# Merge stage: the first four row tiles are formed together, block of features by block of features, with four y buffers

## The chip, the core and the metric

The kernel runs on one core of one Trainium2 chip. The metric is the device time of one execution in microseconds (us). The kernel before took 2590.55 us, the median of three executions (2588.41 to 2590.64).

## What is computed

Two post-norm layers of a streaming encoder over 2048 positions of 1024 features. Each layer ends in the same step: a mixer's gated output is multiplied by an output matrix, the result is added to the scaled residual, and each position is normalised. In the reference:

```
# layer 0 (attention):      h = einsum("bse,ed->bsd", o * silu(gate), w_out)
# layer 1 (RG-LRU):         h = einsum("bse,ed->bsd", y, w_out)
x = layer_norm(DEEPNORM_ALPHA * x + h, ln_g[layer], ln_b[layer])

def layer_norm(x, g, b):
    mu = mean(x);  var = mean(square(x - mu))
    return (x - mu) * rsqrt(var + LN_EPS) * g + b
```

Everything is float32. A float32 product is made of three products of split halves: high times high, high times low, low times high.

## The kernel before

The program is a row of stages, each a block with a barrier at its end: `project`, `attend`, `merge` ("ma"), `project_recur` ("rep"), `merge` again ("rem"). The change touches `merge` alone (lines 796 to 944), which runs twice. It reads the mixer's output as two halves (high and low) laid out features by positions, and the 1024x1024 output matrix, and writes 2048x1024 rows.

Positions are cut into 16 row tiles of 128 (`ST` = 16), features into 8 blocks of 128 (`KC` = 8), output columns into two halves of 512 (`DH` = 2). One row tile takes 8 x 2 x 3 = 48 matmuls and fills two PSUM banks (one `psum[u]`, u = tile mod 4); four such pairs fill all eight banks.

SyncE (queue SP) loads, in this order (lines 841 to 849): weight blocks 0 and 1 (1 MB), y of row tiles 0 and 1 (all 8 feature blocks, both halves, 2 MB, into `yin[0]`), weight blocks 2 and 3, y of tiles 2 and 3 (`yin[1]`), weight blocks 4 and 5, 6 and 7, four tiles of x (0.5 MB each), gain and shift. ScalarE makes the high half of each weight pair (line 908), VectorE the low half (line 920). TensorE then forms tile 0 over all its feature blocks, waiting at each pair of blocks for its split (line 889), then tile 1, and so on: one tile after another, each over all eight blocks.

Behind each tile VectorE adds the residual (line 929), takes the statistics and normalises (lines 933 to 943, with a root on ScalarE), GpSimd multiplies by the gain and adds the shift (lines 877 and 879), and SyncE stores the tile (line 855). After every odd tile n SyncE issues the y of tiles n+3 and n+4 (line 859, 2 MB) right behind the store, then waits until the store has landed (line 861), and reloads the x buffer (line 862). TensorE's tile n waits for its y and for VectorE's sum of tile n-4, which frees its PSUM pair (lines 885 and 886). TensorE, ScalarE, VectorE, GpSimd and SyncE loop over groups of four tiles with a hardware loop.

Of the kernel before, what the change touches and what calls it, by code (L numbers as in the profile page):

```python
# [19 lines left out]
P = 128  # L20
BANK = 512
ALU = mybir.AluOpType
ACT = mybir.ActivationFunctionType
F32 = mybir.dt.float32
F32R = mybir.dt.float32r
# [29 lines left out]
def raw(ap):  # L55

    return ap.bitcast(F32)
# [346 lines left out]
def wait(engine, sem, value):  # L404

    if not isinstance(value, int) or value > 0:
        engine.wait_ge(sem, value)
# [388 lines left out]
def merge(nc, stage, ys, w_out, x, ln_g, ln_b, out):  # L796
# [3 lines left out]
    DH = D // BANK  # L800
# [6 lines left out]
    with ExitStack() as ctx:  # L807
# [1 line left out]
        wst = a.sb("wst", [P, KC, D])  # L809
        wh = a.sb("wh", [P, KC, D], F32R)  # L810
        wl = a.sb("wl", [P, KC, D], F32R)
        yin = [a.sb(f"yin{i}", [P, 2, KC, YW], F32R) for i in range(2)]
        xt = a.sb("xt", [P, RING, D])
        gain = a.sb("gain", [P, D])
        shift = a.sb("shift", [P, D])
# [3 lines left out]
        psum = [a.ps(f"ps{i}", [P, DH, BANK]) for i in range(4)]  # L819

        w_loaded = [a.sem(f"w_loaded{i}") for i in range(WP)]
        p_loaded = a.sem("p_loaded")
        y_loaded = [a.sem(f"y_loaded{i}") for i in range(2)]
        x_loaded = [a.sem(f"x_loaded{i}") for i in range(RING)]
# [14 lines left out]
        @block.sync  # L839
        def _(sp):  # L840
            for h in range(WP):
                part = slice(h * CP, (h + 1) * CP)
                sp.dma_start(wst[:, part, :], w_v[:, part, :]).then_inc(w_loaded[h], 16)  # L843
                if h < 2:
                    sp.dma_start(raw(yin[h][:, :, :, :]), y_v[:, :, :, h * YW:(h + 1) * YW]).then_inc(y_loaded[h], 16)  # L845
            for u in range(RING):
                sp.dma_start(xt[:, u, :], x[u * P:(u + 1) * P, :]).then_inc(x_loaded[u], 16)
            for v, row in ((gain, ln_g), (shift, ln_b)):
                sp.dma_start(v[:, :], row.partition_broadcast(P)).then_inc(p_loaded, 16)

            def tiles(it, last):
                for u in range(RING):
                    n = it * RING + u
                    sp.wait_ge(shifted, n + 1)
                    sp.dma_start(out[bass.ds(n * P, P), :], xt[:, u, :]).then_inc(stored[u], 16)
                    if not last:
                        if u % 2 == 1:
                            b = u // 2
                            sp.dma_start(raw(yin[b][:, :, :, :]), y_v[:, :, :, bass.ds((n + 3) * P, YW)])\
                                .then_inc(y_loaded[b], 16)  # L860
                        sp.wait_ge(stored[u], 16 * (it + 1))
                        sp.dma_start(xt[:, u, :], x[bass.ds((n + RING) * P, P), :]).then_inc(x_loaded[u], 16)

            with sp.Fori(0, ST // RING - 1) as it:
                tiles(it, False)
            tiles(ST // RING - 1, True)
            for u in range(RING):
                sp.wait_ge(stored[u], 16 * (ST // RING))

# [10 lines left out]

        @block.tensor
        def _(pe):
            def tile(it, u):
                n = it * RING + u
                pe.wait_ge(y_loaded[u // 2], 16 * (it + 1))
                wait(pe, summed, n - 3)
                for c in range(KC):
                    if isinstance(it, int) and u == 0 and c % CP == 0:
                        pe.wait_ge(w_split, c // CP + 1)
                    for h in range(DH):  # L890
                        for k, (l, w) in enumerate(((0, wh), (0, wl), (1, wh))):
                            mm = nc.tensor.matmul(psum[u][:, h, :], yin[u // 2][:, l, c, u % 2 * P:(u % 2 + 1) * P],  # L892
                                                  w[:, c, h * BANK:(h + 1) * BANK], start=(c == 0 and k == 0),
                                                  stop=(c == KC - 1 and k == 2))
                mm.then_inc(products, 1)

            for u in range(RING):
                tile(0, u)
            with pe.Fori(1, ST // RING) as it:
                for u in range(RING):  # L900
                    tile(it, u)

        @block.scalar
        def _(act):
            for h in range(WP):
                part = slice(h * CP, (h + 1) * CP)
                act.wait_ge(w_loaded[h], 16)
                nc.scalar.activation(wh[:, part, :], wst[:, part, :], ACT.Copy).then_inc(w_high, 1)  # L908

            with act.Fori(0, ST // RING) as it:  # L910
                for u in range(RING):
                    act.wait_ge(stat, (it * RING + u + 1) * (DH + 2))
                    nc.scalar.activation(rstd[:, u % 2, 0:1], mean_var[:, u % 2, 1:2], ACT.Sqrt).then_inc(rooted, 1)  # L913

        @block.vector
        def _(dve):
            for h in range(WP):
                part = slice(h * CP, (h + 1) * CP)
                dve.wait_ge(w_high, h + 1)
                nc.vector.tensor_tensor(wl[:, part, :], wst[:, part, :], raw(wh[:, part, :]), ALU.subtract)\  # L920
                    .then_inc(w_split, 1)

            with dve.Fori(0, ST // RING) as it:
                for u in range(RING):
# [598 lines left out]
```

## Time and profile before

| | |
|---|---|
| median of 3 executions | 2590.55 us (2588.41 to 2590.64) |
| profiled execution | 2593.75 us, of which the span is 2591.9 us |
| TensorE matmul busy | 2417.6 us (93%), 13921 instructions |
| VectorE, ScalarE, GpSimd busy | 1339.5, 1156.4, 623.0 us |
| mean granted TensorE clock | 0.969 |

A profile is one execution. Its engines are PE (TensorE matmul), PEld (TensorE weight load), DVE (VectorE), ACT (ScalarE), POOL (GpSimd) and SPq (SyncE's queue, which issues the DMAs). Times in the views count from the start of the span. The granted clock is a share of full speed: 1.00 is 2.4 GHz and 0.50 is 1.2 GHz. Matmul starts are recorded, their ends are modelled, so the spacing of starts says more than the duration of one. The first merge lies from 1655 to 1866 us, the second from 2382 to 2592 us.

### The profile page before, as it was taken

What the parts mean: (1) busy time and instruction counts of PE and PEld (TensorE: products, weight loads), DVE (VectorE), ACT (ScalarE), POOL (GpSimd) and SP (SyncE); (2) the same over time, 40 slices, a digit from 0 to 9 for tenths busy, and PEclk for the clock granted to TensorE, in tenths of its full rate; (3) what the DMA queues carried; (4) which work ended last, traced back from release to release, by engine and by line L of the source; (5) the groups of instructions that cost most, each with busy time, mean ns of one, the idle gap of its engine ahead of it and who ended that gap; (6) DMA issues with size and microseconds to landing.
All of it is one profiled execution on the core that took longest, in us unless ns stands there. A gap on an engine that the chain in (4) does not pass through costs nothing. (4 is left out here: it accounts for less than half of the span.)

```text
span 2591.9 us, 41884 instructions
## 1 busy us (share of the span) xinstructions
PE 2417.6 (93%) x13921; PEld 2086.2 (80%) x13921; DVE 1339.5 (52%) x2832; ACT 1156.4 (45%) x2128; POOL 623.0 (24%) x740
## 2 busy tenths in 40 slices
PE   8899999999997999999999999599689999993898
PEld 7688889998876888898888988488578888872786
DVE  4312121211007888888888888433245666574333
ACT  4211111111116888888888888400034556575000
POOL 0000000000002555455545555234300000000244
PEclk9999999999998999999999999799899999996999
DMA  5344343332116445544454444545344354435553
GB/s 182 112 114 130 114 128 107 123 113 86 52 49 146 98 97 126 128 97 96 111 128 111 96 98 95 181 159 194 122 147 122 127 158 130 138 123 168 195 191 135
DMA packets 215772, 325.65 MB, mean 126 GB/s; under 512 B 16097, under 2 KB 141089, under 8 KB 209441
## 3 DMA queue, kind: packets, MB, share of 16 engines
q1 hardware_dynamic: 215136, 323.68, 43.4%
q8 instruction: 53, 0.87, 0.1%
q0 software_dynamic: 512, 0.53, 0.1%
q14 instruction: 71, 0.57, 0.1%
HBM read 197.79 MB, written 126.35 MB: 125 GB/s over the span
## 5 line engine op out<-in xcount | busy, mean ns | idle before, releaser
L760 DVE TENSOR_TENSOR at_pl<-at_tps,at_ph 128x512 fp32r<-128x512 f32 (+3 forms) x640 | 371.0, 604 | 21.7 <-ACT at_ph L705 21.5
L705 ACT ACTIVATE at_ph<-at_tps 128x512 fp32r<-128x512 f32 (+3 forms) x640 | 312.3, 528 | 108.6 <-PE at_tps L627 104.7
L323 ACT ACTIVATE pa_stg<-pa_ps 128x512 fp32r<-128x512 f32 (+1 forms) x128 | 76.2, 597 | 608.1 <-PE pa_ps L227 608.1
L627 PE MATMUL at_tps<-at_ident,at_probs 128*128 128x128 f32 x2176 | 338.3, 273 | 1.4 <-DVE at_pl L760 1.4
L642 PE MATMUL at_ops<-at_ph,at_val 128*128 128x256 f32 (+1 forms) x1152 | 325.1, 304 | 2.0 <-DVE at_pl L760 1.9
L227 PE MATMUL pa_ps<-pa_xh,pa_wh 128*128 128x512 f32 x800 | 312.9, 391 | 12.1 <-DVE pa_stg L390 9.6
L695 ACT ACTIVATE at_probs<-at_probs,at_least 128x128 f32<-128x128 f32 (+15 forms) x256 | 307.1, 1200 | 18.9 <-DVE at_probs L751 18.8
L227 PE MATMUL pa_ps<-pa_xl,pa_wh 128*128 128x512 f32 x800 | 312.2, 390 | 0.0
L227 PE MATMUL pa_ps<-pa_xh,pa_wl 128*128 128x512 f32 x800 | 312.2, 390 | 0.0
L612 PE MATMUL at_sps<-at_k,at_q 128*128 128x512 f32 (+3 forms) x640 | 272.2, 425 | 26.1 <-DMA at_k<-forget_sums 22.1
L642 PE MATMUL at_ops<-at_pl,at_val 128*128 128x256 f32 (+1 forms) x1152 | 294.8, 281 | 0.0
L627 PEld LDWEIGHTS at_tps<-at_ident,at_probs 128*128 128x128 f32 x2176 | 256.1, 141 | 25.0 <-DVE at_pl L760 6.8
L751 DVE TENSOR_SCALAR_CACHE_REDUCE at_probs<-at_sps,at_least 128x512 f32<-128x512 f32 (+3 forms) x384 | 248.2, 646 | 16.7 <-PE at_sps L613 0.5
L613 PE MATMUL at_sps<-at_k,at_q 68*128 68x512 f32 (+3 forms) x640 | 233.4, 368 | 0.0
L642 PEld LDWEIGHTS at_ops<-at_ph,at_val 128*128 128x128 f32 x1152 | 220.5, 191 | 12.2 <-issue 2.5
L642 PEld LDWEIGHTS at_ops<-at_pl,at_val 128*128 128x128 f32 x1152 | 219.8, 191 | 8.3
L1230 PE MATMUL rep_ps<-rep_xh,rep_wh 128*128 128x512 f32 x512 | 201.6, 394 | 2.9 <-DVE rep_wl L1369 2.9
L751 DVE TENSOR_SCALAR_CACHE_REDUCE at_probs<-at_sps 128x512 f32<-128x512 f32 (+3 forms) x256 | 162.1, 633 | 79.2 <-PE at_sps L613 54.9
L892 PE MATMUL rem_ps<-rem_wh,rem_yin 128*128 128x512 f32 x512 | 161.9, 397 | 43.3 <-DMA rem_yin<-y_gated 36.4
L1230 PE MATMUL rep_ps<-rep_xh,rep_wl 128*128 128x512 f32 x512 | 200.6, 392 | 0.0
L1230 PE MATMUL rep_ps<-rep_xl,rep_wh 128*128 128x512 f32 x512 | 200.4, 391 | 0.0
L393 DVE TENSOR_TENSOR pa_stg<-pa_ps,pa_stg 128x512 fp32r<-128x512 f32 x64 | 44.3, 691 | 286.5 <-ACT pa_stg L323 286.5
(165 smaller groups left out, 4664.2 us busy)
## 6 DMA issues: line engine op xcount, KB each, us to landing
at_q<-q_halves SPq DMA_DIRECT2D x48, 512.0 KB
at_k<-k_halves SPq DMA_DIRECT2D x48, 512.0 KB
pa_wst<-in_attn_w_in SPq DMA_DIRECT2D x16, 1024.0 KB, 7.2
q_halves<-pa_stg SPq DMA_DIRECT2D x32, 512.0 KB, 3.7
k_halves<-pa_stg SPq DMA_DIRECT2D x32, 512.0 KB, 3.7
v_halves<-pa_stg SPq DMA_DIRECT2D x32, 512.0 KB, 2.8
at_val<-v_halves SPq DMA_DIRECT2D x16, 1024.0 KB, 16.8
ma_yin<-y_halves SPq DMA_DIRECT2D x8, 2048.0 KB, 9.0
```

The source lines that it names most:

```text
L227: mm = nc.tensor.matmul(out, lhs[p](c), rhs[q](c), start=(c == 0 and k == 0), stop=(c == KC - 1 and k == 2))
L323: nc.scalar.activation(out, source(kind, s), func, scale=scale).then_inc(evac_h, 1)
L612: nc.tensor.matmul(out, q1[hp][:, i * P:(i + 1) * P], k1[hp][:, keys], start=True, stop=False)
L613: mm = nc.tensor.matmul(out, q2[hp][0:K, i * P:(i + 1) * P], k2[hp][0:K, keys], start=False, stop=not last)
L627: mm = nc.tensor.transpose(tps[c % TB][:, k, :], probs[s % ROWS][:, t0:t0 + P], ident[:, :])
L642: mm = nc.tensor.matmul(ops[b][:, 0, c0:GW], val[hp][:, kt, :], t[b][:, kt, c0:GW], start=(kt == 0 and t is ph), stop=(kt == KT - 1 and t ...
L695: nc.scalar.activation(probs[s % ROWS][:, 0:w], probs[s % ROWS][:, 0:w], ACT.Exp, bias=least[:, s % ROWS, n_chunks[s] - 1:n_chunks[s]], sc ...
L705: nc.scalar.activation(ph[g % 2][:, j * PB:j * PB + n, i % 2 * P:(i % 2 + 1) * P], tps[c % TB][:, 0:n, :], ACT.Copy).then_inc(high_out, 1)
L751: nc.vector.tensor_scalar(probs[s % ROWS][:, j * BANK:j * BANK + w], sps[c % SB][:, 0:w], 1.0, least[:, s % ROWS, j - 1:j] if j else None, ...
L760: nc.vector.tensor_tensor(pl[g % 2][at], tps[c % TB][:, 0:n, :], raw(ph[g % 2][at]), ALU.subtract)\
L892: mm = nc.tensor.matmul(psum[u][:, h, :], yin[u // 2][:, l, c, u % 2 * P:(u % 2 + 1) * P], w[:, c, h * BANK:(h + 1) * BANK], start=(c == 0 ...
L1230: mm = nc.tensor.matmul(psum[t % RING][:, :], wt[:, b, k, :], xt[:, k, at], start=(k == 0 and m == 0), stop=(k == KC - 1 and m == 2))
```

## The change

Weights are loaded in single blocks of 128 features, and so is the y of the first four tiles: for each pair of blocks two weight transfers (0.5 MB each), then four y transfers (one block, two tiles, both halves: 0.25 MB each). TensorE forms tiles 0 to 3 together: for block 0 all four tiles' products, then block 1, and so on, with all eight PSUM banks open. The weight split is made block by block (8 steps each on ScalarE and VectorE, where there were 4). There are four y buffers; y of tiles 4 to 7 is issued in front, behind x, gain and shift. After that y of tiles n+3 and n+4 is issued after odd tiles n = 5, 7, 9, 11, and now behind the x reload, so behind the wait for the store. TensorE's and SyncE's loops over tiles are written out.

```diff
-        yin = [a.sb(f"yin{i}", [P, 2, KC, YW], F32R) for i in range(2)]
+        yin = [a.sb(f"yin{i}", [P, 2, KC, YW], F32R) for i in range(4)]
...
+        y_first = [a.sem(f"y_first{i}") for i in range(WP)]
...
             for h in range(WP):
-                part = slice(h * CP, (h + 1) * CP)
-                sp.dma_start(wst[:, part, :], w_v[:, part, :]).then_inc(w_loaded[h], 16)
-                if h < 2:
-                    sp.dma_start(raw(yin[h][:, :, :, :]), y_v[:, :, :, h * YW:(h + 1) * YW]).then_inc(y_loaded[h], 16)
+                for c in range(h * CP, (h + 1) * CP):
+                    sp.dma_start(wst[:, c, :], w_v[:, c, :]).then_inc(w_loaded[h], 16)
+                for c in range(h * CP, (h + 1) * CP):
+                    for b in range(2):
+                        sp.dma_start(raw(yin[b][:, :, c, :]), y_v[:, :, c, b * YW:(b + 1) * YW]).then_inc(y_first[h], 16)
...
-            def tiles(it, last):
-                for u in range(RING):
-                    n = it * RING + u
-                    sp.wait_ge(shifted, n + 1)
-                    sp.dma_start(out[bass.ds(n * P, P), :], xt[:, u, :]).then_inc(stored[u], 16)
-                    if not last:
-                        if u % 2 == 1:
-                            b = u // 2
-                            sp.dma_start(raw(yin[b][:, :, :, :]), y_v[:, :, :, bass.ds((n + 3) * P, YW)])\
-                                .then_inc(y_loaded[b], 16)
-                        sp.wait_ge(stored[u], 16 * (it + 1))
-                        sp.dma_start(xt[:, u, :], x[bass.ds((n + RING) * P, P), :]).then_inc(x_loaded[u], 16)
...
+            def load_y(j):
+                sp.dma_start(raw(yin[j % 4][:, :, :, :]), y_v[:, :, :, j * YW:(j + 1) * YW]).then_inc(y_loaded[j % 2], 16)
+
+            load_y(2)
+            load_y(3)
+            for n in range(ST):
+                u = n % RING
+                sp.wait_ge(shifted, n + 1)
+                sp.dma_start(out[n * P:(n + 1) * P, :], xt[:, u, :]).then_inc(stored[u], 16)
+                if n + RING < ST:
+                    sp.wait_ge(stored[u], 16 * (n // RING + 1))
+                    sp.dma_start(xt[:, u, :], x[(n + RING) * P:(n + RING + 1) * P, :]).then_inc(x_loaded[u], 16)
+                if n % 2 == 1 and RING <= n < ST - RING:
+                    load_y((n + 3) // 2)
...
+            def part(n, c):
+                u = n % RING
+                for h in range(DH):
+                    for k, (l, w) in enumerate(((0, wh), (0, wl), (1, wh))):
+                        mm = nc.tensor.matmul(psum[u][:, h, :], yin[n // 2 % 4][:, l, c, n % 2 * P:(n % 2 + 1) * P],
+                                              w[:, c, h * BANK:(h + 1) * BANK], start=(c == 0 and k == 0),
+                                              stop=(c == KC - 1 and k == 2))
+                return mm
+
+            def tile(n):
+                pe.wait_ge(y_loaded[n // 2 % 2], 16 * (n // RING))
+                pe.wait_ge(summed, n - 3)
                 for c in range(KC):
...
+                    mm = part(n, c)
                 mm.then_inc(products, 1)
...
+            for c in range(KC):
+                pe.wait_ge(w_split, c + 1)
+                pe.wait_ge(y_first[c // CP], 32 * CP)
                 for u in range(RING):
-                    tile(it, u)
+                    mm = part(u, c)
+                    if c == KC - 1:
+                        mm.then_inc(products, 1)
+            for n in range(RING, ST):
+                tile(n)
...
+            for c in range(KC):
+                act.wait_ge(w_loaded[c // CP], 16 * CP)
+                nc.scalar.activation(wh[:, c, :], wst[:, c, :], ACT.Copy).then_inc(w_high, 1)
...
+            for c in range(KC):
+                dve.wait_ge(w_high, c + 1)
+                nc.vector.tensor_tensor(wl[:, c, :], wst[:, c, :], raw(wh[:, c, :]), ALU.subtract).then_inc(w_split, 1)
```

## Rows read from the trace of the kernel before

**Rows 1.** The page's costliest groups: busy us, mean ns, idle before, releaser.
```profile
L892 PE MATMUL rem_ps<-rem_wh,rem_yin 128*128 128x512 f32 x512 | 161.9, 397 | 43.3 <-DMA rem_yin<-y_gated 36.4
```

**Rows 2.** TensorE's waits: who waited for whom, us in total, times, longest.
```profile
PE rem_ps L892 <- DMA rem_yin<-y_gated: 36.4, 1, 36.4
...
PE ma_ps L892 <- DMA ma_yin<-y_halves: 19.5, 1, 19.5
...
PE ma_ps L892 <- DVE ma_wl L920: 8.3, 2, 7.0
...
PE rem_ps L892 <- DVE rem_wl L920: 6.9, 2, 5.6
```

**Rows 3.** Timeline, head of the first merge: start, us, engine, line, operation.
```profile
1655.14 0.40 SPq L843 DMA_DIRECT2D ma_wst<-in_attn_w_out  x1
1655.60 0.45 SPq L845 DMA_DIRECT2D ma_yin<-y_halves  x1
...
1660.12 1.91 ACT L908 ACTIVATE ma_wh<-ma_wst 128x2048 fp32r<-128x2048 f32 x1 [12.30 <-DMA ma_wst<-in_attn_w_out]
...
1662.07 2.29 DVE L920 TENSOR_TENSOR ma_wl<-ma_wst,ma_wh 128x2048 fp32r<-128x2048 f32 x1 [19.78 <-ACT ma_wh L908]
1666.13 0.29 PEld L892 LDWEIGHTS ma_ps<-ma_wh,ma_yin 128*128 128x128 f32 x1 [19.77 <-DMA ma_yin<-y_halves]
...
1672.99 0.50 PE L892 MATMUL ma_ps<-ma_wh,ma_yin 128*128 128x512 f32 x1 [1.37 <-DVE ma_wl L920]
...
1683.01 0.79 PE L892 MATMUL ma_ps<-ma_wh,ma_yin 128*128 128x512 f32 x1 [6.98 <-DVE ma_wl L920]
```

**Rows 4.** Windows, first merge: busy (count) per engine, granted clock, DMA share, GB/s.
```profile
1655.00:1660.00 5.00, 0.00 (x0) 0.00 (x0) 0.00 (x0) 0.00 (x0) 0.00 (x0) 0.50 0.75 245
1660.00:1665.00 5.00, 0.00 (x0) 0.00 (x0) 2.29 (x1) 1.91 (x1) 0.00 (x0) 0.50 1.10 356
1665.00:1670.00 5.00, 3.87 (x9) 3.09 (x10) 0.00 (x0) 1.29 (x1) 0.00 (x0) 0.50 1.06 380
1670.00:1675.00 5.00, 3.63 (x13) 2.36 (x13) 2.29 (x1) 0.61 (x1) 0.00 (x0) 0.78 1.09 363
...
1685.00:1690.00 5.00, 5.00 (x22) 4.09 (x21) 0.52 (x1) 0.00 (x0) 0.00 (x0) 0.91 0.37 147
```

**Rows 5.** The chain that ended last, head of the second merge: start, us, what.
```profile
2382.25 0.38 SPq L843
...
2408.68 170.94 PE rem_ps L892 x744
2579.63 0.02 issue
2579.65 1.23 DVE rem_xt L929
```

**Rows 6.** Timeline: residual sums of tiles 0, 1 and 15, and tile 0's gain.
```profile
1690.11 1.22 DVE L929 SCALAR_TENSOR_TENSOR ma_xt<-ma_xt,ma_ps 128x1024 f32<-128x1024 f32 x1 [4.59 <-PE ma_ps L892]
...
1694.55 2.39 POOL L877 TENSOR_TENSOR ma_xt<-ma_xt,ma_gain 128x1024 f32<-128x1024 f32 x1 [42.98 <-DVE ma_xt L943]
...
1700.99 1.22 DVE L929 SCALAR_TENSOR_TENSOR ma_xt<-ma_xt,ma_ps 128x1024 f32<-128x1024 f32 x1 [6.51 <-PE ma_ps L892]
...
1853.31 1.22 DVE L929 SCALAR_TENSOR_TENSOR ma_xt<-ma_xt,ma_ps 128x1024 f32<-128x1024 f32 x1 [6.51 <-PE ma_ps L892]
```

**Rows 7.** Timeline of SyncE's queue: stores, x reloads and y refill behind tiles 0 and 1.
```profile
1699.60 0.37 SPq L855 DMA_DIRECT2D x<-ma_xt  x1
1702.42 0.35 SPq L862 DMA_DIRECT2D ma_xt<-in_x  x1
1710.47 0.35 SPq L855 DMA_DIRECT2D x<-ma_xt  x1
1711.01 0.39 SPq L859 DMA_DIRECT2D ma_yin<-y_halves  x1
```

**Rows 8.** Line L859, all 12 y refills of both merges: issue to landing.
```profile
DMA to landing us min/median/max: 8.8/8.9/10.2
```

**Rows 9.** Windows at the program's start, where x comes in 0.5 MB transfers.
```profile
6.00:9.00 3.00, 3.00 (x16) 2.98 (x15) 2.43 (x5) 2.24 (x4) 0.00 (x0) 1.00 1.01 379
9.00:12.00 3.00, 1.90 (x13) 1.52 (x11) 2.53 (x5) 2.18 (x5) 0.00 (x0) 1.00 1.07 379
```

More of the change, by code:

```diff
@@ L849, in _ @@
                 sp.dma_start(v[:, :], row.partition_broadcast(P)).then_inc(p_loaded, 16)
-            def tiles(it, last):
-                for u in range(RING):
-                    n = it * RING + u
-                    sp.wait_ge(shifted, n + 1)
-                    sp.dma_start(out[bass.ds(n * P, P), :], xt[:, u, :]).then_inc(stored[u], 16)
-                    if not last:
-                        if u % 2 == 1:
-                            b = u // 2
-                            sp.dma_start(raw(yin[b][:, :, :, :]), y_v[:, :, :, bass.ds((n + 3) * P, YW)])\
-                                .then_inc(y_loaded[b], 16)
-                        sp.wait_ge(stored[u], 16 * (it + 1))
-                        sp.dma_start(xt[:, u, :], x[bass.ds((n + RING) * P, P), :]).then_inc(x_loaded[u], 16)
-            with sp.Fori(0, ST // RING - 1) as it:
-                tiles(it, False)
-            tiles(ST // RING - 1, True)
+            def load_y(j):
[11 more added lines that the diff above has]
+                    load_y((n + 3) // 2)
             for u in range(RING):
@@ L882, in _ @@
         def _(pe):
[L883 to L886, printed above, removed]
-                for c in range(KC):
[L888 to L894, printed above, removed]
+            def part(n, c):
[6 more added lines that the diff above has]
+                return mm
@@ L895, in tile @@
+            def tile(n):
+                pe.wait_ge(y_loaded[n // 2 % 2], 16 * (n // RING))
+                pe.wait_ge(summed, n - 3)
+                for c in range(KC):
+                    mm = part(n, c)
                 mm.then_inc(products, 1)
-            for u in range(RING):
-                tile(0, u)
-            with pe.Fori(1, ST // RING) as it:
+            for c in range(KC):
+                pe.wait_ge(w_split, c + 1)
+                pe.wait_ge(y_first[c // CP], 32 * CP)
                 for u in range(RING):
-                    tile(it, u)
+                    mm = part(u, c)
+                    if c == KC - 1:
+                        mm.then_inc(products, 1)
@@ L903, in _ @@
+            for n in range(RING, ST):
+                tile(n)
         @block.scalar
         def _(act):
[L905 to L908, printed above, removed]
+            for c in range(KC):
+                act.wait_ge(w_loaded[c // CP], 16 * CP)
+                nc.scalar.activation(wh[:, c, :], wst[:, c, :], ACT.Copy).then_inc(w_high, 1)
@@ L916, in _ @@
         def _(dve):
[L917 to L921, printed above, removed]
+            for c in range(KC):
+                dve.wait_ge(w_high, c + 1)
+                nc.vector.tensor_tensor(wl[:, c, :], wst[:, c, :], raw(wh[:, c, :]), ALU.subtract).then_inc(w_split, 1)
             with dve.Fori(0, ST // RING) as it:
```

## The prediction

> **What bounds the kernel now.** I began with the page. TensorE is busy 93% of the span, so only time in which it stands still, or runs at the low clock, is there to be won; the page's group for line 892 shows 43.3 us of idle time in the second merge alone [rows 1]. TensorE's waits say what that is: it waits once per merge for y, and twice per merge for the split of the weights [rows 2]. The long y waits (36.4 and 19.5 us) are mostly the end of the stage before and the barrier; what the change can reach begins with the merge's first DMA issue, at 1655.14 and 2382.25. So I went to the timeline of the head. TensorE starts at 1666.13, 11.0 us after the first issue, runs two feature blocks of tile 0, starts the next two at 1672.99 and the last four only at 1683.01 [rows 3]. The windows show why: until 1675 the DMA engines are full (share 1.06 to 1.10, 356 to 380 GB/s) [rows 4], and tile 0 needs all the weights, the last in the queue. From there on nothing stops TensorE: the residual sums of tiles 0 and 15 start at 1690.11 and 1853.31, 163.20 us for 15 tiles, 10.88 us a tile, and tiles 0 to 1 show the same 10.88 [rows 6]. The second merge is alike: after the weights' last wait, one unbroken piece of TensorE work, 744 of the 768 matmuls, from 2408.68 to 2579.63 [rows 5]. The tail behind the last product (sum, norm, gain, shift, store) is untouched.
>
> In sum: 16 tiles are 16 x 10.88 = 174.1 us of work at the full clock. The first merge takes 1853.31 - 1655.14 = 198.2 us from first issue to last product, the second 2579.65 - 2382.25 = 197.4 us. So 24.1 and 23.3 us are start, gaps and low clock.
>
> **The start.** The change moves TensorE's first matmul to where one pair of blocks has landed: weights 1.05 MB and y 1.05 MB, 2.10 MB in all, instead of 3.15 MB. By 1660 some 5 x 0.245 = 1.23 MB have moved, by 1665 3.01 MB [rows 4], by 1666.13 (1.13 us at 0.380) 3.43 MB, when the 3.15 MB asked for have landed [rows 3]; 0.28 MB of later transfers lay between them. With the same 0.28 MB the new first pair has landed when 2.38 MB have moved: 1660 + (2.38 - 1.23) / 0.356 = 1663.2, 8.1 us after the first issue. The split isn't in the way: the first weights land at 1660.12, ScalarE takes 1.91 and VectorE 2.29 us for two blocks [rows 3], so about half for one: block 0 is split near 1660.1 + 1.0 + 1.2 = 1662.3, block 1 near 1663.5, while block 0 holds TensorE 24 matmuls, 5.4 us and more. Eight short steps instead of four long ones cost nothing behind that cover; without it they cost their fixed parts, under a us.
>
> **The gaps.** Afterwards each pair of blocks is 48 matmuls, 10.9 us of TensorE time, and takes 2.10 MB / 0.36 to 0.38 = 5.5 to 5.8 us to arrive. The transfers gain 5 us a pair and both gaps go. Behind the 8.4 MB stand 2 MB of x, 1 MB of gain and shift and now 4.2 MB of y for tiles 4 to 7: 15.7 MB at 0.38 are 41 us, done near 1698, needed from 1663.2 + 2.3 + 4 x 10.88 = 1709. The 24 head issues (6 before) cost 0.40 to 0.45 us each [rows 3], 10.5 us, less than the 22 us in which their bytes move.
>
> The kernel before runs tile 0 in three bursts with waits between them, and the clock is 0.50 until 1670 and low again at 1683 [rows 3, 4]; after the change a burst (10.9 us) is longer than the arrival behind it (5.5 to 5.8), so there should be one burst only. A rule of the Trainium skill (TensorE: Matmul & The Clock Gate, HAM oscillation) speaks against the new shape: do all K-tiles of one row tile before waiting for data, since short bursts between DMA waits bring the low clock back, and the change does one K block of four tiles at a time. By that rule the low clock would return at each later pair; that is rival F.
>
> **The clock.** The head before is slow twice. From 1666.13 the granted clock is 0.50, with 0.78 as mean of 1670 to 1675: 2.2 us more, so 6.1 us at half. At 1683.01, after 7 us of rest, it is low again until 1685.9 (0.91 as mean of 1685 to 1690) [rows 3, 4]: 2.9 us. The loss shows directly: 744 matmuls from 1683.01 at 10.88/48 us end at 1851.65, the sum starts at 1853.31, 1.7 us later; in the second merge 2408.68 + 168.64 = 2577.32 against 2579.65, 2.3 us. After the change there is one slow stretch: between 1.7 us and half of 6.1, 3.1 us. I take 2.3.
>
> **Ends.** First merge: 1663.2 + 174.1 + 2.3 = 1839.6 for 1853.31, 13.7 us. Second: 2382.25 + 8.1 + 174.1 + 2.3 = 2566.8 for 2579.65, 12.9 us. Together 26.6 us, with both ends' rows in [rows 3, 5, 6].
>
> **PSUM and the post-processing.** In the last feature block each tile takes 6 matmuls, so the first four tiles end 6 x 10.88/48 = 1.36 us apart and not 10.88; tile 0's last product comes 18 matmuls, 4.1 us, before tile 3's. Tile 4 needs tile 0's sum, 1.22 us [rows 6]: covered with 2.8 us to spare. VectorE needs some 4.4 us a tile (1690.11 to GpSimd's start at 1694.55), GpSimd 4.8: counted from tile 0's last product, GpSimd ends tiles 0 to 3 near 9.4, 14.2, 19.1 and 23.9, and tile 5's product comes at 4.1 + 21.8 = 25.9. The queue has drained by then; SyncE's store, wait and reload of 3.2 us a tile fit too.
>
> **The y refill.** This is the new wait. Before, y of tiles n+3 and n+4 is issued 10.02 us after tile n's product (1711.01 - 1700.99), lands 8.9 us later [rows 6 to 8], and is needed 2 x 10.88 = 21.76 us after it: 2.8 us to spare. After, it stands behind the wait for the store and the x reload: store at 9.48, reload 2.82 later as for tile 0 (1702.42 - 1699.60) [rows 7], then y some 0.4 us later: 12.7, landing at 21.6, with 0.1 us to spare. Queued behind that wait on SyncE are y and nothing else urgent. Though there are four buffers, the refill is no earlier. The slowest refill took 10.2 [rows 8], which would be 1.2 us late. A late refill gives the next pair as much slack, so only two of the four refills of a merge can be late by the whole amount d: cost 2d a merge, 0 to 2 x 1.2. I take 0.5 us for both merges together, and 4.8 as the bound.
>
> Loops written out: tile ends 10.88 us apart are exactly 48 spacings of a loop body, so TensorE's loop costs nothing now and its removal gives nothing.
>
> **Sum.** 26.6 - 0.5 = 26.1 us. The profiled execution took 2593.75 us, span 2591.9 and 1.85 around it; less 26.1 that is 2567.6. The median of the executions lies 3.2 below the profiled one: 2590.55 - 26.1 = 2564.5.
>
> **Rivals.**
> A, late start. If the small transfers are slower or land interleaved with the next pair's, TensorE starts later. Price: if its first pair needs what 4.2 MB took before, it starts where the second pair of weights landed, about 1668.7 (split 4.3 us before 1672.99), 5.5 us late, two times: gain 26.1 - 11 = 15, 2575.5; halfway, gain 20.6, 2570. For it: a block of y is a quarter of a MB, and no row has that size in a stream. Against: 0.5 MB transfers in a row run at 379 GB/s [rows 9], as the large ones do. The Trainium skill (DMA: Bandwidth & Descriptors, Measured) asks for transfers of 1 MiB or more for 75% of the peak; 379 GB/s in 0.5 MB pieces doesn't bear it out for a stream.
> B, late refills. All at 10.2 us to landing: d = 1.1, cost 2 x 2 x 1.1 = 4.4, and for each wait perhaps a lower clock: gain 22, 2568.5.
> C, slower than before. The same refill behind x: if reload and refill hinder each other so that y lands d late, the cost is 4d in all; it eats the 26.6 us at d = 6.7 and is a loss over 0.2% (5.2 us) at d = 8, y landing 17 us after its issue. Price at d = 8: +5.4, 2596. Against: no refill took over 10.2.
> D, the change doesn't do what it says: the pieces are issued singly, but they land all together and TensorE stands until nearly the last, near 1683. Then all 768 matmuls come behind 1683 and not 744, and 24 x 10.88/48 = 5.4 us are lost per merge: 2590.5 + 10.9 = 2601; a start up to 5.4 us before that is no loss, 2590.
> F, low clock at each pair. If TensorE comes to stand between pairs long enough, each of the three later pairs of a merge costs a slow stretch of at least 1.7 us, 2 x 3 x 1.7 = 10.2 in all: gain 15.9, 2574.7. Against: it needs a pair to arrive later than 10.9 us behind the last one, and the arrivals take half of that [rows 4]. It is the skill's rule named above.
> E, better than forecast: start at 1662.4 (2.10 MB exactly), clock loss 1.7, no late refill: 26.6 + 2 x (0.8 + 0.6) = 29.4, 2561.
>
> **How the numbers follow.** Forecast, 2564.5 with its own 2562 to 2567: 0.48. E: 0.12. B: 0.14. A: 0.17. F: 0.02. C: 0.03. D: 0.04. The range runs from 2560 (E and the spread of executions, 1.5) to 2573 (B, and A past its middle), and leaves out about one in ten. A measurement tells about 0.2%, 5.2 us, from no change. Faster 0.93 (forecast, E, B, A, F), same 0.03 (part of C and D), slower 0.04.
>
> **What would show it.** In the profile after: the merge's first matmul 8.1 us behind its first weight issue; no gap until the last product; tile 4's first matmul without a wait; one stretch at half clock per merge; a wait for y at tile 8 under 1 us; last products near 1839.6 in the first merge and, with the time won there taken off, near 2566.8 - 13.7 = 2553.1 in the second. A start after 1666 would break the first step, y waits at tiles 8 and 12 over 1.2 us the refill step, a second low clock the clock step.

## The result, and the profile after

The changed kernel takes 2577.75 us (median of 6 executions, 2574.78 to 2579.05), the kernel before on the same chip 2590.6 us (6 executions). The ratio is 0.9946, 95% interval 0.9936 to 0.9957: 12.85 us faster, where 26.1 were forecast, and outside the range of 2560 to 2573. The direction is right, half of the gain is missing. Two executions far off all others (6372 us of the kernel before and 10166 us of before_refill_behind) are left out of the ratios below.

The profiled execution took 2578.18 us, with a span of 2576.3. Its timeline at the head of the first merge (start, us, engine, line, operation), to be read against [rows 3]:

```profile
1654.58 0.93 SPq L844 DMA_DIRECT2D ma_wst<-in_attn_w_out  x2
1655.55 1.99 SPq L847 DMA_DIRECT2D ma_yin<-y_halves  x4
1657.58 3.35 SPq L844 DMA_DIRECT2D ma_wst<-in_attn_w_out  x2
1659.84 2.01 ACT L913 ACTIVATE ma_wh<-ma_wst 128x1024 fp32r<-128x1024 f32 x2 [12.57 <-DMA ma_wst<-in_attn_w_out]
...
1667.46 0.77 PE L887 MATMUL ma_ps<-ma_wh,ma_yin 128*128 128x512 f32 x1 [21.42 <-DMA ma_yin<-y_halves]
```

TensorE starts 12.9 us behind the first issue. It was 11.0 before and forecast at 8.1. In the second merge it starts at 2385.81, 11.5 us behind the first issue at 2374.30. The first weights still arrive some 5 us behind the issue; it is y that is late. TensorE's start lies behind 1666, which the prediction named as the sign that its first step is broken. The windows (busy per engine, granted clock, DMA share, GB/s) answer to [rows 4]; the last line is of the second merge:

```profile
1655.00:1660.00 5.00, 0.00 (x0) 0.00 (x0) 0.00 (x0) 0.16 (x1) 0.00 (x0) 0.50 0.77 246
1660.00:1665.00 5.00, 0.00 (x0) 0.00 (x0) 2.36 (x2) 1.84 (x2) 0.00 (x0) 0.50 0.94 244
1665.00:1670.00 5.00, 2.54 (x6) 2.10 (x7) 0.00 (x0) 0.10 (x1) 0.00 (x0) 0.50 0.98 323
1670.00:1675.00 5.00, 5.00 (x17) 3.93 (x17) 2.36 (x2) 1.90 (x2) 0.00 (x0) 0.69 1.01 334
...
2379.00:2384.00 5.00, 0.00 (x0) 0.00 (x0) 2.36 (x2) 2.01 (x2) 0.00 (x0) 0.50 0.79 213
```

Where 356 GB/s flowed before, 244 and 213 flow now, and the DMA engines are busy for 0.94 and 0.79, not 1.10. From its first matmul to its wait at tile 8 TensorE has no gap, as forecast. The next loss stands in the timeline of VectorE's tile sums (line 932). From tile 5 on, spacings longer than 10.88 us are what to look for, as in [rows 6]; the lines are those of tiles 0, 4, 5, 7, 8 and 15:

```profile
1709.86 1.22 DVE L932 SCALAR_TENSOR_TENSOR ma_xt<-ma_xt,ma_ps 128x1024 f32<-128x1024 f32 x1 [23.79 <-PE ma_ps L887]
...
1730.66 1.21 DVE L932 SCALAR_TENSOR_TENSOR ma_xt<-ma_xt,ma_ps 128x1024 f32<-128x1024 f32 x1
1736.17 1.21 DVE L932 SCALAR_TENSOR_TENSOR ma_xt<-ma_xt,ma_ps 128x1024 f32<-128x1024 f32 x1
...
1757.46 1.22 DVE L932 SCALAR_TENSOR_TENSOR ma_xt<-ma_xt,ma_ps 128x1024 f32<-128x1024 f32 x1 [6.52 <-PE ma_ps L887]
1770.37 1.22 DVE L932 SCALAR_TENSOR_TENSOR ma_xt<-ma_xt,ma_ps 128x1024 f32<-128x1024 f32 x1 [8.54 <-PE ma_ps L887]
...
1847.93 1.22 DVE L932 SCALAR_TENSOR_TENSOR ma_xt<-ma_xt,ma_ps 128x1024 f32<-128x1024 f32 x1 [6.52 <-PE ma_ps L887]
```

The step from tile 7 to tile 8 is 12.91 us, 2.03 too long. Tiles 12 and 14 are 0.21 and 1.19 late too, tile 8 of the second merge 1.88 and its tile 14 0.04. TensorE's own row at tile 8 names the refill:

```profile
1757.03 0.39 PE L887 MATMUL ma_ps<-ma_wh,ma_yin 128*128 128x512 f32 x1
1759.13 0.50 PE L887 MATMUL ma_ps<-ma_wh,ma_yin 128*128 128x512 f32 x1 [1.71 <-DMA ma_yin<-y_halves]
```

The sum of the merges fits the medians. From first issue to last sum the first merge takes 1847.93 - 1654.58 = 193.35 us (198.17 before), the second 2564.04 - 2374.30 = 189.74 (197.40): 4.8 and 7.7, together 12.5 us of the 12.85. The two profiles' spans differ by 3 us more, outside the two stretches from first issue to last sum.

| term, both merges | forecast | measured | missing |
|---|---|---|---|
| start behind the first issue | 8.1 + 8.1 | 12.9 + 11.5 | 8.2 |
| late refills | 0.5 | 3.4 + 1.9 | 4.8 |
| low clock (rest of first matmul to last sum, less 174.1) | 2.3 + 2.3 | 3.0 + 2.2 | 0.6 |

### The profile page after: what moved, and what is told of

It reads as the page before. It is cut to its first block and busy times, and to the rows that moved or that the text cites. A ratio compares the mean times of both kernels' runs of the same rounds, so it can differ in the third digit from the quotient of the medians.

```text
span 2576.3 us, 41772 instructions
## 1 busy us (share of the span) xinstructions
PE 2410.6 (94%) x13921; PEld 2081.1 (81%) x13921; DVE 1350.7 (52%) x2840; ACT 1160.1 (45%) x2136; POOL 623.2 (24%) x740
## 5 line engine op out<-in xcount | busy, mean ns | idle before, releaser
L227 PE MATMUL pa_ps<-pa_xh,pa_wh 128*128 128x512 f32 x800 | 313.1, 391 | 12.1 <-DVE pa_stg L390 9.6
```

What stands on the lines that cost most here:

```text
L227: mm = nc.tensor.matmul(out, lhs[p](c), rhs[q](c), start=(c == 0 and k == 0), stop=(c == KC - 1 and k == 2))
```

## Experiments

Each kernel is compared with the kernel before on its own chip; where a text gives a time against the changed kernel, it is the difference of medians, though all but after_padded_again ran on chips where the kernel before took 1.0 us less (2589.5 to 2589.6). The table shows, from each profile, the first matmul behind the first issue and the summed lateness of tiles 4 to 15, for both merges.

| kernel | median us | ratio to before (95%) | start | tiles late |
|---|---|---|---|---|
| changed kernel | 2577.75 | 0.9946 (0.9936 to 0.9957) | 12.9, 11.5 | 3.4, 1.9 |
| refill_early | 2570.93 | 0.9927 (0.9913 to 0.9940) | 12.8, 12.0 | 0, 0 |
| gpsimd_light | 2575.89 | 0.9942 (0.9927 to 0.9958) | 13.4, 12.0 | 0.6, 4.1 |
| head_large | 2572.37 | 0.9932 (0.9919 to 0.9946) | 11.6, 9.4 | 3.3, 1.9 |
| before_split_y | 2591.39 | 1.0008 (0.9998 to 1.0017) | 12.9, 12.1 | 0, 0 |
| large_early | 2568.13 | 0.9917 (0.9903 to 0.9930) | 11.7, 9.4 | 0, 0 |
| pitch_padded | 2563.17 | 0.9896 (0.9881 to 0.9911) | 8.3, 8.2 | 0, 0 |
| before_refill_behind | 2595.55 | 1.0022 (1.0012 to 1.0031) | 11.0, 11.1 | 2.5, 1.9 |
| before_padded | 2589.14 | 0.9997 (0.9988 to 1.0007) | 11.2, 11.6 | 0, 0 |
| after_padded | 2569.16 | 0.9917 (0.9901 to 0.9934) | 10.1, 10.1 | 4.3, 1.5 |
| after_padded_again | 2566.47 | 0.9907 (0.9879 to 0.9936) | 8.4, 8.4 | 3.4, 1.6 |
| halves_apart | 2570.93 | 0.9929 (0.9912 to 0.9946) | 13.0, 11.6 | 0, 0 |
| padded_large | 2561.96 | 0.9895 (0.9880 to 0.9910) | 7.8, 7.7 | 0, 0 |

**refill_early.** The four buffers are used; the refills of tiles 8 to 15 stand behind tiles 1, 3, 5 and 7, in front of the wait for the store. They count on other semaphores than in the changed kernel, and TensorE's wait follows (these lines are left out).

```diff
...
                 sp.dma_start(out[n * P:(n + 1) * P, :], xt[:, u, :]).then_inc(stored[u], 16)
+                if n % 2 == 1 and n < ST // 2:
+                    load_y((n + 7) // 2)
                 if n + RING < ST:
...
-                if n % 2 == 1 and RING <= n < ST - RING:
-                    load_y((n + 3) // 2)
...
```

> The changed kernel with the y refills of tiles 8 to 15 moved: y of tiles 8 and 9 is issued after tile 1's store and ahead of the wait for it, then one after tiles 3, 5 and 7, so that the four buffers are used. Theory (late refills): TensorE's waits at tiles 8, 12 and 14 (2.0, 0.2 and 1.2 us in the first merge, 1.9 at tile 8 in the second) vanish and the time falls by 5.3 us, to 2572.5. The start of each merge stays late (12.9 and 11.5 us behind the first issue). Rival (the waits stand for contention among the transfers, which comes with any refill): waits of 1 to 2 us turn up at other tiles and the time stays within 1 us of 2577.75.

All waits behind the head are gone: from first matmul to last sum 175.8 and 176.0 us, which is 174.1 and 1.7 and 1.9 us of low clock. The time falls by 6.8 us (5.9 if each is taken against the kernel before on its own chip), a little more than the 5.3 of the profile's lateness. Late refills are shown as one of the two losses, and contention that comes with any refill is out as their cause. The early refills do have a price, which lies elsewhere: x reloads are issued up to 9.4 us behind their store and not 2.6 to 4.5, and in the first merge tile 5's sum waits 1.9 us for its x. The pause before tile 6's product, 4.8 us for VectorE in the changed kernel, absorbs it.

**gpsimd_light.** The gain and shift of tiles 0 to 5 on 8 columns only; GpSimd's loop is written out for it.

```diff
...
+                w = 8 if n < 6 else D
...
-                    nc.gpsimd.tensor_tensor(xt[:, u, :], xt[:, u, :], gain[:, :], ALU.mult).then_inc(gained, 1)
+                nc.gpsimd.tensor_tensor(xt[:, u, :w], xt[:, u, :w], gain[:, :w], ALU.mult).then_inc(gained, 1)
```

> The changed kernel, but gain and shift are applied to 8 of 1024 columns in tiles 0 to 5 of each merge (that part of the output is left out). Theory (VectorE and GpSimd slow each other down while they work at the same time, which they did not do before): VectorE's normalising step behind tiles 1 to 5 takes 0.81 us and not 2.05, the residual sums of tiles 0 to 4 stand 4.3 us apart and not 5.5, tile 5's store is issued some 5 us earlier, and the wait at tile 8 is gone: time 3 to 5 us lower. Rival (the normalising step is long because sums queue up in front of it): 2.05 us stays.

The mechanism holds for the normalising step. That step of tile 1, of the changed kernel and then of this one (timeline of VectorE):

```profile
1717.69 2.04 DVE L946 TENSOR_SCALAR ma_xt<-ma_xt,ma_mean_var,ma_rstd 128x1024 f32<-128x1024 f32 x1
```

```profile
1715.76 0.81 DVE L946 TENSOR_SCALAR ma_xt<-ma_xt,ma_mean_var,ma_rstd 128x1024 f32<-128x1024 f32 x1
```

The sums of tiles 0 to 4 stand 4.27 us apart and not 5.51, and tile 8 starts without a wait in both merges. The time does not follow: 1.9 us less, not 3 to 5. In the profile another refill was late: in the second merge tile 7's store, issued at 2480.13, landed late, and with the refill behind it tile 10 came 4.04 us late. SyncE's queue there:

```profile
2480.13 0.34 SPq L861 DMA_DIRECT2D out<-rem_xt  x1
2484.59 0.32 SPq L864 DMA_DIRECT2D rem_xt<-x  x1
2484.96 0.44 SPq L854 DMA_DIRECT2D rem_yin<-y_gated  x1
```

4.46 us passed from store to reload, where most reloads of this kernel's later tiles took 2.6: a refill behind the wait carries each swing of the store. What delayed this store no run tells. The wait itself was 2.11 us. The rest of the 4.04 is a fresh start and the low clock, which came back here and behind no other refill of these profiles. The window (TensorE busy, granted clock, DMA share, GB/s) and, below it, the one behind the wait of 2.07 us at tile 14 of after_padded:

```profile
2495.00:2500.00 5.00, 5.00 (x17) 0.66 0.33 107
```

```profile
1820.00:1825.00 5.00, 2.93 (x13) 1.00 0.32 124
```

At a mean of 0.66 five microseconds lose 1.7 us of work. So this kernel shows that GpSimd's overlap makes the wait at tile 8, and its time says little about what that wait costs.

**before_refill_behind.** The kernel before with the refill moved behind the reload, nothing else.

```diff
...
-                        if u % 2 == 1:
-                            b = u // 2
-                            sp.dma_start(raw(yin[b][:, :, :, :]), y_v[:, :, :, bass.ds((n + 3) * P, YW)])\
-                                .then_inc(y_loaded[b], 16)
                         sp.wait_ge(stored[u], 16 * (it + 1))
                         sp.dma_start(xt[:, u, :], x[bass.ds((n + RING) * P, P), :]).then_inc(x_loaded[u], 16)
+                        if u % 2 == 1:
+                            b = u // 2
+                            sp.dma_start(raw(yin[b][:, :, :, :]), y_v[:, :, :, bass.ds((n + 3) * P, YW)])\
+                                .then_inc(y_loaded[b], 16)
```

> The kernel before with one edit: the y refill is issued behind the wait for the store and the x reload, as in the changed kernel. Theory of the prediction (the place alone leaves 0.1 us to spare): waits of 0 to 0.5 us at tiles 4, 8 and 12, in all under 2 us in both merges, ratio 1.000 to 1.001; the wait of 2 us at tile 8 in the changed kernel then needs VectorE's backlog as well. Rival (the place alone costs it): 2 us at every second pair, 6 to 8 us in all, ratio 1.0025 or more.

Neither expectation holds. The refill is issued 12.81 us behind the product (1712.50 - 1699.69), as worked out, and lands 9.1 us later in the median (8.7 to 9.7) and not 8.9. That leaves the 0.1 us to spare negative. TensorE's waits are short, and yet the sums come 0.6 to 0.8 us late at six of the twelve pairs and 0.3 at one, 4.4 us in all: a short wait costs more than itself. The waits of TensorE in the first merge, us in total, times, longest:

```profile
PE ma_ps L892 <- DMA ma_yin<-y_halves: 1.2, 4, 0.4
```

Four waits of 0.3 on average against 2.5 us of lateness, some 0.3 us for each fresh start. So the place alone costs 4.4 us in the profile and 1.0022 in the ratio, whose interval reaches the rival's 1.0025; the medians lie 6.0 us apart, of which the lateness covers all but 1.6.

**before_split_y.** The kernel before, with each of the two 2 MB transfers of y at the head in 8 pieces.

```diff
...
-                    sp.dma_start(raw(yin[h][:, :, :, :]), y_v[:, :, :, h * YW:(h + 1) * YW]).then_inc(y_loaded[h], 16)
+                    for c in range(KC):
+                        sp.dma_start(raw(yin[h][:, :, c, :]), y_v[:, :, c, h * YW:(h + 1) * YW]).then_inc(y_first[h], 16)
...
```

> The kernel before, with the y of tiles 0 and 1 and of tiles 2 and 3 loaded in 8 transfers of one block (0.25 MB) each, not in one of 2 MB; nothing else is changed, TensorE still works tile by tile. Theory (small transfers): y of tiles 0 and 1 lands 2 to 4 us later than 11.0 us behind the first issue, each merge starts and ends that much later at most, ratio 1.000 to 1.003. Rival (the order of y and weights): start at 11.0 us as before, ratio 1.000, and the DMA share stays at 1.05 to 1.10.

The same bytes in the same order arrive 1.9 and 1.1 us later, and the rate dips for the first four microseconds of y only. Windows of the first merge:

```profile
1655.00:1657.00 2.00, 0.00 (x0) 0.00 (x0) 0.00 (x0) 0.00 (x0) 0.00 (x0) 0.50 0.98 395
1657.00:1659.00 2.00, 0.00 (x0) 0.00 (x0) 0.00 (x0) 0.89 (x1) 0.00 (x0) 0.50 0.86 245
1659.00:1661.00 2.00, 0.00 (x0) 0.00 (x0) 0.95 (x1) 1.02 (x1) 0.00 (x0) 0.50 0.92 259
1661.00:1663.00 2.00, 0.00 (x0) 0.00 (x0) 1.34 (x1) 0.00 (x0) 0.00 (x0) 0.50 1.08 360
```

So cutting y into single blocks costs by itself, without TensorE's new order. But the dip ends at 1661, when half of these blocks are still to come: from 1661 to 1665 four more single-block transfers of y are issued and 365 GB/s flow. A single block read from rows 8 KB apart is thus not slow at all times. The later start hardly counts here, since the last weights set this kernel's end: 1.0008.

**head_large.** Three transfers per pair of blocks and not six: weights 1 MB, y of each block for all four tiles 0.5 MB. The first two y buffers lie side by side, and the waits follow (these lines are left out).

```diff
...
-                for c in range(h * CP, (h + 1) * CP):
-                    sp.dma_start(wst[:, c, :], w_v[:, c, :]).then_inc(w_loaded[h], 16)
+                part = slice(h * CP, (h + 1) * CP)
+                sp.dma_start(wst[:, part, :], w_v[:, part, :]).then_inc(w_loaded[h], 16)
                 for c in range(h * CP, (h + 1) * CP):
-                    for b in range(2):
-                        sp.dma_start(raw(yin[b][:, :, c, :]), y_v[:, :, c, b * YW:(b + 1) * YW]).then_inc(y_first[h], 16)
+                    sp.dma_start(raw(yf[:, :, c, :]), y_v[:, :, c, 0:2 * YW]).then_inc(y_first[h], 16)
...
```

> The changed kernel with the same bytes in the same order for each pair of blocks, in 3 transfers and not 6: the two weight blocks in one of 1 MB, and each y block for all four tiles in one of 0.5 MB with rows of 2 KB (the first two y buffers lie side by side). Theory (small transfers let the 16 DMA engines drift apart and stand still, so that the last engine finishes the first pair late): the windows behind the first weights show the DMA share back at 1.0 or more (0.94 and 0.79 now), the first matmul comes 8 to 9 us behind the first issue and not 12.9 and 11.5, time 6 to 8 us lower, 2570 to 2572. Rival (the first pair is late because its y was just written or because single blocks lie badly in memory): start still 11 to 13 us behind the issue, time as now.

The time falls by 5.4 us, less than the theory wanted, and the start by 1.3 and 2.1 only. The windows spoke against it: once y begins, transfers of twice the size dip as deep, though for a shorter time. Second merge:

```profile
2376.00:2378.00 2.00, 0.00 (x0) 0.00 (x0) 0.00 (x0) 0.36 (x1) 0.00 (x0) 0.50 1.00 373
2378.00:2380.00 2.00, 0.00 (x0) 0.00 (x0) 1.27 (x2) 1.65 (x2) 0.00 (x0) 0.50 0.71 185
2380.00:2382.00 2.00, 0.00 (x1) 0.03 (x1) 1.09 (x1) 0.00 (x0) 0.00 (x0) 0.50 0.96 370
```

185 GB/s with rows of 2 KB in 0.5 MB transfers; the changed kernel, with rows of 1 KB in 0.25 MB, had 241, 170 and 259 GB/s in the three windows from 2378.00. Twice the size does not lift the rate in the dip (187 GB/s at its lowest in the first merge), it shortens the dip. My theory of small transfers fell here as the main cause. What both have in common is where they read: 128 rows of one block, 8 KB apart.

**large_early** joins both repairs.

> Both repairs at once: the 3 larger transfers per pair of blocks of head_large and the early refills of refill_early. If the two losses (late start, late refills) are separate, the gains add: start as in head_large (11.6 and 9.4 us behind the first issue), no wait behind it, 175.8 us from first to last product: 2571 less some 3.5, 2567 to 2568. Rival (head_large's gain came from something else than the start): 2570 to 2571 as refill_early.

2568.13 us and the starts of head_large, without late tiles: 9.6 us under the changed kernel, of the 12.2 that separate losses would add up to (6.8 + 5.4). The profiles show both repairs side by side; the medians show most of the sum.

**pitch_padded.** refill_early with one more edit, in the memory layout of y; it is read and written as before.

```diff
...
-    qs, ks, ys = (dram(n, (2, D, S)) for n in ("q_halves", "k_halves", "y_halves"))
+    qs, ks = (dram(n, (2, D, S)) for n in ("q_halves", "k_halves"))
+    ys = dram("y_halves", (2, D, S + 256))[:, :, 0:S]
...
-    ys = nc.dram_tensor("y_gated", (2, D, S), F32, kind="Internal").ap()
+    ys = nc.dram_tensor("y_gated", (2, D, S + 256), F32, kind="Internal").ap()[:, :, 0:S]
```

> refill_early, with the rows of the y tensor in memory 9 KB apart instead of 8 KB (256 unused positions behind each row); transfers, order and sizes as in refill_early. Theory M (the transfers of single blocks are slow because rows 8 KB apart, in two halves 8 MB apart, meet in the same part of the memory: the rate is 150 to 250 GB/s in that stretch in small and in large transfers alike): the rate there goes to 350 GB/s or more, the first matmul comes 8.5 to 9.5 us behind the first issue, the time falls by 5 to 7 us against refill_early, to 2564 to 2566. Theory S (the number and size of the transfers): start at 12 to 13 us, time as refill_early, 2571, give or take 1.

Theory M's numbers came: 2563.17 us, 7.8 less than refill_early, with the starts at 8.3 and 8.2 us, where the prediction had 8.1. Second merge, three windows from 1.6 us behind the first issue:

```profile
2366.00:2368.00 2.00, 0.00 (x0) 0.00 (x0) 0.00 (x0) 0.00 (x0) 0.00 (x0) 0.50 1.00 383
2368.00:2370.00 2.00, 0.00 (x0) 0.00 (x0) 0.00 (x0) 0.75 (x1) 0.00 (x0) 0.50 1.00 339
2370.00:2372.00 2.00, 0.00 (x0) 0.00 (x0) 1.67 (x2) 1.25 (x2) 0.00 (x0) 0.50 1.07 373
```

The same windows of refill_early, whose first issue was at 2367.36:

```profile
2369.00:2371.00 2.00, 0.00 (x0) 0.00 (x0) 0.00 (x0) 0.00 (x0) 0.00 (x0) 0.50 0.99 377
2371.00:2373.00 2.00, 0.00 (x0) 0.00 (x0) 0.00 (x0) 0.91 (x1) 0.00 (x0) 0.50 0.69 193
2373.00:2375.00 2.00, 0.00 (x0) 0.00 (x0) 1.82 (x2) 1.09 (x2) 0.00 (x0) 0.50 0.77 151
```

Same transfers, same sizes, same order; 193 and 151 GB/s become 339 and 373. In the first merge the two windows of 2 us from 3.6 us behind the first issue have 180 and 170 against 277 and 372: a short dip is left even with padding. The first pair of blocks had been issued by 2.8 to 3.0 us behind the first issue in both kernels, so issuing does not explain the difference.

**before_padded** gives the padding to the kernel before.

> The kernel before with the rows of the y tensor 9 KB apart and no other edit. Its y comes in transfers of 2 MB at 350 GB/s already. Theory M (8 KB rows hurt only where a transfer holds one block, so that all 16 engines read the same few rows' ends at once): first matmul 10.5 to 11.0 us behind the first issue as now, ratio 0.999 to 1.000. Rival (the row pitch is a loss everywhere, and padding alone brings the 7 us): ratio 0.997.

No difference (0.9997), start 11.2 and 11.6 us. The transfers that hold all blocks gain nothing from the padding.

**after_padded** is the changed kernel with padding alone, profiled twice.

> The changed kernel with the rows of the y tensor 9 KB apart and no other edit; its refills stay behind the x reload. If start and refills are two separate losses: first matmul 8.2 to 8.4 us behind the issue, waits at tile 8 and others 2 to 5 us in all as in the changed kernel, time 2577.75 less some 7 to 8, 2570. This is the prediction's 2564.5 with only its refill step wrong. Rival (padding also speeds up the refills' transfers, 8.9 us to landing, and takes the waits away): 2565.

> The same kernel as after_padded, profiled once more, because its profile showed a start of 10.1 us where pitch_padded, whose head is the same, showed 8.3 and 8.2, and because that profiled execution was above the median of its runs. If the start varies from execution to execution: 8.2 to 9 us now and a shorter profiled execution, 2568 to 2570. If the head of this kernel is really slower: 10 us again.

The first profile has starts of 10.1 us, and is the slowest of that kernel's executions (2572.31; the others 2567.14 to 2569.38). The second has 8.4 and 8.4, and 2566.47 is the median of two executions only. The start of this head varies by 2 us between executions even with padding. The rate is nearly the same in both profiles: 2.38 MB have moved by 8.0 and 8.1 us behind the first issue in the one, by 7.7 and 7.8 in the other. What differs is how much of later transfers went ahead of the first pair's last piece (below); why, no run tells. The medians are 8.6 and 11.3 us below the changed kernel's, and the late tiles stay, 5.8 and 5.0 us: padding repairs the start, in one profile only in part, and nothing of the refills.

**halves_apart.** refill_early, 8 KB rows, the two halves 8 MB + 16 KB apart and not 8 MB; each refill comes in two transfers of 1 MB (these lines are left out).

```diff
...
-    qs, ks, ys = (dram(n, (2, D, S)) for n in ("q_halves", "k_halves", "y_halves"))
+    qs, ks = (dram(n, (2, D, S)) for n in ("q_halves", "k_halves"))
+    ys = dram("y_halves", (2, D + 2, S))[:, 0:D, :]
...
-    ys = nc.dram_tensor("y_gated", (2, D, S), F32, kind="Internal").ap()
+    ys = nc.dram_tensor("y_gated", (2, D + 2, S), F32, kind="Internal").ap()[:, 0:D, :]
```

> refill_early with y rows 8 KB apart as before, but the low half moved 16 KB further off from the high half than 8 MB; the refills come as two transfers of 1 MB. Theory R (the rows of one half meet each other): start still 12 to 13 us behind the issue, 2571. Theory H (the two halves of one row, exactly 8 MB apart, meet): start 8.5 to 9.5 us, 2564 to 2566.

Theory R holds: 2570.93 us like refill_early, starts 13.0 and 11.6. Moving the halves against each other changes nothing; with pitch_padded that leaves the distance of the rows within a half.

**padded_large** has padding, larger transfers and early refills.

> Padded rows, 3 transfers per pair of blocks and early refills together. If with padded rows the size of the transfers no longer counts: 2563, start 8.0 to 8.3 us. If small transfers cost something of their own as well (the 1.2 and 2.1 us that head_large won): start 7.5 us or earlier and 2561 to 2562.

2561.96 us is in the range of the second expectation, the starts of 7.8 and 7.7 us lie between the two. Ratio to the kernel before 0.9895: it beats both kernels, 27.6 us under the kernel before and 15.8 under the changed one. Its step from pitch_padded is 1.2 us, less than these comparisons can tell; the starts, 0.5 and 0.6 us earlier, point the same way, to a small cost of small transfers of their own.

## Why the prediction was wrong

**The place of the gain was right.** The two gaps of tile 0 are gone, TensorE runs from its first matmul to tile 8 without a wait, one stretch at 1.2 GHz is left per merge, and the low clock costs 3.0 and 2.2 us for 2.3 and 2.3. The rule of the Trainium skill that rival F takes up (TensorE: Matmul & The Clock Gate, HAM oscillation) did not apply: a burst of 10.9 us per pair outlasts the arrival even at the reduced rate (2.1 MB at 244 GB/s are 8.6 us), and no second low stretch is seen. PSUM was free in time, and writing out the loops brought nothing visible.

**The start: the term was mis-sized, 8.2 of the 13.6 us that are missing.** I put the first pair at 8.1 us by giving 2.1 MB of single blocks the 356 GB/s of the 2 MB transfer [rows 4], and by letting 0.28 MB of later transfers pass in between, as before. Neither held. The rate: windows of 0.5 us, added up, show 2.38 MB moved by 10.1 us behind the first issue in both merges, not 8.1. The order: TensorE did not start then, but when more had moved. The window from first issue to first matmul (TensorE busy, granted clock, DMA share, GB/s), for both merges of the changed kernel, then the first merges of pitch_padded and after_padded:

```profile
1654.58:1667.46 12.88, 0.00 (x0) 0.50 0.85 254
2374.30:2385.81 11.51, 0.00 (x0) 0.50 0.82 256
```

```profile
1653.97:1662.28 8.31, 0.00 (x0) 0.50 0.87 307
```

```profile
1653.30:1663.37 10.07, 0.00 (x0) 0.50 0.89 318
```

12.88 x 0.254 = 3.27 MB and 2.95 MB had moved when the 2.10 MB asked for were complete: 1.17 and 0.85 MB of later transfers lay between them, where I had 0.28. So of the 8.2 us the lower rate has some 4.0 and the later transfers in between some 4.2 (2.7 and 1.4). With padding 2.55 MB sufficed in pitch_padded, at the forecast rate; in the first profile of after_padded the rate is the forecast's too, but 3.20 MB had to move, which is its start of 10.1 us. Against rival A I argued with 379 GB/s in 0.5 MB pieces of x [rows 9]. Those rows show the size of a transfer and not its place: x is read in whole 4 KB rows, one behind the other, y in 1 KB of every 8 KB. Nor is it x alone that moves in them: 1071 of the 1370 packets are under 2 KB, mostly those of a 1 MB weight transfer issued at 4.14. The runs separate size and place. With the size alone enlarged 1.3 and 2.1 us come back (head_large), with the pitch alone changed 4.5 and 3.7 against refill_early (pitch_padded); after_padded against the changed kernel has 2.8 and 1.4 in one profile, 4.5 and 3.1 in the other. Rival A named the right place, a late start by single blocks of y, and both causes, slower transfers and pieces that land among the next pair's; its price of 5.5 us per merge was near the 4.8 and 3.4 measured; its chance of 0.17 was too small, and no case joined A with late refills, which is what happened.

What lies behind the lower rate is inferred: in a transfer of one block all 16 DMA engines read rows 8 KB apart in the same 1 MB of each half, and they would meet there. With rows 9 KB apart, or with all blocks in one transfer, the slow stretch is short or absent. The Trainium skill (DMA: Bandwidth & Descriptors, Latency and other measured facts) reports for copies that a row pitch of 512 KiB gave 207 GB/s, 2 MiB 164 and 4 MiB 103, that 4 KiB of padding restored the full rate at 4 MiB, and gives streams that meet in the same memory channels in step as its unverified inference. Here the pitch is 8 KB and 1 KB of padding was enough, which is outside what the page gives; the direction agrees. I had not drawn on it, since its sizes lie far off. SyncE's queue shows the stall too: two issues of the next weights took 3.35 us in the changed kernel, at 1657.58, and 1.05 us (1656.86) in pitch_padded.

**The refills: 4.8 us missing, three steps wrong.** First, the landing: 8.9 us was taken from refills that had the store in front of them; behind a reload they took 9.1 in before_refill_behind and 9.1 to 10.4 in the changed kernel. Second, "some 4.4 us a tile" for VectorE: that is its time with GpSimd idle. In the backlog of tiles 0 to 4 both work at once, the normalising step takes 2.04 and not 0.81, and tiles stand 5.5 us apart. The queue had not drained at tile 5: its sum starts 0.5 us behind its product (1746.58 - 10.88 = 1735.70, against 1736.17), its norm takes 1.2 us longer, and the refill is issued at 1749.70, 14.0 us behind the product and not 12.7. 14.0 + 9.4 = 23.4 against 21.76: 1.64 us late, and the wait is 1.71. Third, a fresh start costs TensorE 0.3 us on top (a wait of 1.71, a tile 2.03 late). The range had 4.8 as its bound for the refills and the profile shows 5.3. The alternation that I claimed (a late refill gives slack to the next) is seen in the second merge, where tile 8 alone is late; in the first, tiles 12 and 14 are late.

On the second step the Trainium skill (SBUF — State Buffer, SBUF: two separate sides) says that VectorE and GpSimd share a pair of ports, held for a whole instruction by one of them. The trace agrees in direction: 0.81 us alone, 2.04 to 2.05 beside GpSimd's steps of 2.40, 0.81 again in gpsimd_light, while the sum, which reads PSUM, keeps 1.21 to 1.22. Whether the step is held up for all of GpSimd's or shares with it, these durations don't show.

**The sum.** 26.1 - 8.2 - 4.8 - 0.6 = 12.5, measured 12.85. With both losses repaired the kernel takes 2563.17 us (pitch_padded) where 2564.5 was forecast, with starts of 8.3 and 8.2 us for 8.1 and no late refill for 0.5: the sum was that of a kernel whose y is laid out and refilled otherwise.

**What stays open.** That the pitch of 8 KB takes part is shown by the padded kernels; why is not. Whether the 16 DMA engines wait for the memory itself or for each other isn't told apart by any run, 9 KB is the only other pitch tried, so that nothing here singles out powers of two, and before_split_y moves single blocks of the same pitch at 365 GB/s once its first ones are through: something at the beginning of y is needed as well. Nor does any run show what lets later transfers get ahead of the first pair, by 0.4 MB in one execution and 1.1 MB in another of the same kernel; that the padded kernels mostly have less of it may or may not be the padding's doing.

## What to carry to other kernels

When a large transfer is cut so that work can begin early, the first piece must be priced from a row with the same pattern of addresses, not only of the same size, and the bytes queued behind it may get in front of its last piece; where the pieces read short runs from rows a fixed distance apart, try another pitch along with the cut. A transfer that has 0.1 us to spare by rows of another situation has none: put refills ahead of waits, above all when buffers were added for them. Where a change makes tiles finish together, the engines behind them overlap for the first time, and their durations from the quiet trace no longer hold.

## What the hardware showed beyond that

In the four microseconds from 3.6 us behind the first issue (windows of 2 us), y in single-block transfers of 0.25 MB from rows 8 KB apart moved, together with weights, at 135 to 238 GB/s (changed kernel, refill_early, gpsimd_light, halves_apart), the same transfers from rows 9 KB apart at 277 to 394 (pitch_padded and both profiles of after_padded). Later single blocks from rows 8 KB apart moved at 365 GB/s (before_split_y, 1661 to 1665). When 2.10 MB asked for first on one queue were complete, between 2.46 MB (padded_large) and 3.35 MB (gpsimd_light) had moved.

A wait of 0.3 us on average delayed TensorE's tile by 0.6. Behind a wait of 2.11 us the granted clock fell to a mean of 0.66 over five microseconds (gpsimd_light), behind one of 2.07 us it stayed at 1.00 (after_padded). In the changed kernel a store issued 6.2 us behind a 2 MB refill was followed by its reload, which waits for the store, only after 4.46 and 4.34 us; behind most other stores it took 2.6.
